# Routing logits by token: the activations as TensorE's stationary operand, the bias added in the same three banks

## What is computed

```
def hier_moe(u, lp):
    x = u.reshape(-1, dm)
    lg = (x @ lp['rt_grp_w'] + lp['rt_grp_b']).astype(F32)
    pg = jax.nn.softmax(lg, axis=-1)
    sel = jnp.argmax(lg, axis=-1)
    ...
    le = (x @ lp['rt_exp_w'] + lp['rt_exp_b']).astype(F32).reshape(-1, N_GROUPS, EXP_PER_GROUP)
```

## Time and profile before

| | |
|---|---|
| median of 3 runs | 1442.87 us (1442.4 to 1446.44) |
| the profiled execution's own time | 1438.41 us |
| span in its profile | 1436.6 us |
| TensorE's mean granted clock in it | 0.929 of 2.4 GHz |
| TensorE busy with matmuls | 1212.6 us |
| VectorE busy | 498.1 us |
| ScalarE busy | 277.2 us |

### The profile page before, as it was taken

The page is one execution under the profiler, slowest core; times in us unless marked ns, Lnnn a source line. Parts: engine busy times, 40 slices in busy tenths (PEclk is TensorE's granted clock), DMA queues, the critical chain, the costliest instruction groups (busy, mean ns, idle before and its releaser), DMA issues. The chain is left out here.

```text
span 1436.6 us, 27279 instructions
## 1 busy us (share of the span) xinstructions
PE 1212.6 (84%) x12154; PEld 784.3 (55%) x12154; DVE 498.1 (35%) x1275; ACT 277.2 (19%) x683; POOL 37.0 (3%) x65
## 2 busy tenths in 40 slices
PE   3789876678788889999978999588789899999974
PEld 3455554667775455455434555368785465455432
DVE  0103058352635260111115033956753350110113
ACT  2012053221320121011001124333320121011002
POOL 2000000000000020000000000000000000000000
PEclk9799986999999989999998999689998989999997
DMA  9754460335251417775716232000001307775711
GB/s 353 208 207 153 171 235 1 127 113 199 84 141 36 140 31 236 250 246 204 234 61 182 90 90 74 1 2 4 9 4 55 121 7 248 255 242 186 246 48 44
DMA packets 135678, 191.74 MB, mean 133 GB/s; under 512 B 16563, under 2 KB 100768, under 8 KB 135168
## 3 DMA queue, kind: packets, MB, share of 16 engines
q1 hardware_dynamic: 132256, 179.32, 38.1%
q0 software_dynamic: 2032, 6.23, 1.4%
q10 hardware_dynamic: 1264, 4.33, 0.8%
HBM read 187.63 MB, written 2.23 MB: 132 GB/s over the span
## 5 line engine op out<-in xcount | busy, mean ns | idle before, releaser
L1125 PE MATMUL bank<-ring,region 128*128 128x512 f32 x512 | 224.8, 593 | 0.0
L1205 ACT ACTIVATE region<-bank 128x256 f32<-128x256 f32 (+5 forms) x318 | 128.8, 430 | 422.9 <-PE bank L1146 105.8
L1125 PEld LDWEIGHTS bank<-ring,region 128*128 128x128 f32 x512 | 96.0, 190 | 112.4 <-issue 110.8
L1961 DVE SCALAR_TENSOR_TENSOR region<-region,bank 128x256 f32<-128x256 f32 x32 | 15.4, 480 | 334.2 <-ACT region L1462 334.2
L1146 PE MATMUL bank<-ring,region 128*128 128x512 f32 x256 | 111.2, 593 | 0.0
L1771 DVE COPY_PREDICATED region<-lev,bank 128x512 f32<-128x512 uint8 (+1 forms) x90 | 61.1, 679 | 121.1 <-PE bank L772 120.6
L967 PE MATMUL bank<-u,ring 128*128 128x384 f32 x288 | 94.9, 487 | 0.0
L1556 DVE SCALAR_TENSOR_TENSOR h<-bank,mod,h 128x128 f32<-128x128 f32 (+1 forms) x160 | 56.4, 411 | 103.8 <-PE bank L1041 62.4
L1041 PE MATMUL bank<-u,ring 128*128 128x384 f32 x256 | 86.4, 500 | 5.9 <-DVE u L1854 5.9
L1146 PEld LDWEIGHTS bank<-ring,region 128*128 128x128 f32 x256 | 48.1, 190 | 57.3 <-issue 57.3
L876 PE MATMUL bank<-ring,cond 128*32 128x128 f32 x1536 | 51.6, 284 | 28.1 <-issue 14.7
(11 more groups left out here) (268 smaller groups left out, 1523.6 us busy)
## 6 DMA issues: line engine op xcount, KB each, us to landing
ring<-in_moe_w SPq DMA_DIRECT2D x96, 1024.0 KB, 6.5
ring<-in_w_mod SPq DMA_DIRECT2D x48, 1024.0 KB, 8.4
ring<-in_w_in SPq DMA_DIRECT2D x20, 768.0 KB, 9.1
ring<-in_w_in SPq DMA_DIRECT2D x12, 256.0 KB, 6.1
region<-in_bands POOLq DMA_DIRECT2D x2, 1280.0 KB, 7.7
ring<-in_w_out SPq DMA_DIRECT2D x4, 576.0 KB, 4.2
ring<-in_w_out SPq DMA_DIRECT2D x8, 288.0 KB, 6.1
ring<-in_w_out SPq DMA_DIRECT2D x6, 384.0 KB, 6.3
```

Source lines behind the costliest of these rows:

```text
L1125: last = pe.matmul(bank[j % 2][:, :], xs[:, job % 2, c, :], w[:, c, :], start=(c == 0), stop=(c == KT - 1))
L1205: return act.activation(dst, src, ACT.Copy)
```

## The change

The operands of the logits' matmuls change places. The stationary operand is now a tile of the activations, `u[:, c, tc(t)]` (128 channels by 128 tokens), and the moving one is `route_w[:, c, :]`, 20 columns. The logits come out by token, 128 partitions by 20, in bank 5 + t for token tile t. The bias's matmul of ones with `route_b` is added to the same accumulation. ScalarE's copy, its two semaphores, the buffer `logits` and the three matmuls with the identity go. Since banks 5, 6 and 7 now hold logits when `u` is transposed, the six groups of transposes go round banks 0 to 4, and the sixth waits until ScalarE has copied the first. VectorE's copy of the logits reads 20 columns of each of three banks instead of 60 of one.

```
@@ -1067,20 +1065,19 @@
                 for c in range(KT):
                     pe.wait_ge(u_up, 2 * KT * l + KT + c + 1)
-                    last = pe.matmul(bank[7][0:20, 0:T], route_w[:, c, :], u[:, c, :], start=(c == 0), stop=(c == KT - 1))
-                last.then_inc(logit_mm, 1)
-                pe.wait_ge(logit_cp, l + 1)
+                    for t in range(NT):
+                        pe.matmul(bank[5 + t][:, 0:20], u[:, c, tc(t)], route_w[:, c, :], start=(c == 0), stop=False)
                 for t in range(NT):
-                    dst = bank[7][:, t * 20:(t + 1) * 20]
-                    pe.matmul(dst, logits[:, tc(t)], ident[0:20, 0:20], start=True, stop=False)
-                    last = pe.matmul(dst, ones_row, route_b[:, :], start=False, stop=True)
+                    last = pe.matmul(bank[5 + t][:, 0:20], ones_row, route_b[:, :], start=False, stop=True)
                 last.then_inc(route_mm, 1)
 
 
                 for g in range(2 * NT):
                     t, half = g // 2, g % 2
+                    if g == 5:
+                        pe.wait_ge(utok_cp, 2 * NT * l + 1)
                     for q in range(4):
-                        last = pe.transpose(bank[g][:, tc(q)], u[:, 4 * half + q, tc(t)], ident)
+                        last = pe.transpose(bank[g % 5][:, tc(q)], u[:, 4 * half + q, tc(t)], ident)
                     last.then_inc(utok_mm, 1)
 
                 pe.wait_ge(onehot_up, l + 1)
@@ -1433,12 +1430,10 @@
                 norm(l, 0)
-                act.wait_ge(logit_mm, l + 1)
-                copy(logits, bank[7][0:20, 0:T]).then_inc(logit_cp, 1)
                 for g in range(2 * NT):
                     t, half = g // 2, g % 2
                     act.wait_ge(utok_mm, 2 * NT * l + g + 1)
-                    copy(u_tok[:, t, 512 * half:512 * half + 512], bank[g][:, :]).then_inc(utok_cp, 1)
+                    copy(u_tok[:, t, 512 * half:512 * half + 512], bank[g % 5][:, :]).then_inc(utok_cp, 1)
@@ -1880,7 +1875,7 @@
                 dve.wait_ge(route_mm, l + 1)
-                link(dve.tensor_copy(rl, bank[7][:, 0:20 * NT].rearrange("p (t n) -> p t n", t=NT)))
+                link(dve.tensor_copy(rl, psum[:, 5:5 + NT, 0:20]))
```

More of the change, by code:

```diff
@@ L283, in build @@
         xs = view(2, KT, P)
-        logits = view(T)[0:20, :]
         silu = view(2, DE)
@@ L323, in build @@
         modt_mm = sem("modt_mm")
-        logit_mm, logit_cp = sem("logit_mm"), sem("logit_cp")
         route_mm, utok_mm, rank_mm, hid_mm, down_mm = (sem("route_mm"), sem("utok_mm"), sem("rank_mm"),
```

## The result

The changed kernel takes 1448.46 us, the median of 11 runs (1442.45 to 1452.45), against 1443.62 for the kernel before in 11 runs beside it. The ratio is 1.0034 with a 95% interval of 1.0018 to 1.0050, so it is slower by 4.9 us, between 2.6 and 7.2. I had forecast the side and the clock in the logits, but 11.1 us.

What follows compares the result with a forecast made beforehand. It took TensorE to bound the kernel, its matmuls filling 84% of the span. Averaging 7.0 and 13.4 us gave 10.2, plus 0.9 for the gather 11.1, on 1442.9: 1454.0 us, range 1446 to 1460.

Steps and rivals of the forecast that it cites:

- with a rise: Case where the clock rises late in the transposes, so rank matmuls run at full clock; 3.3 and 3.7 us by layer.
- without: Case where the clock stays at 0.50 through transposes and rank matmuls; 6.5 and 6.9 us by layer.
- the price of 11.6 us: Logits and bias: 54 records at 0.215 us, clock at 0.50 throughout, up to the first transpose; +1.5 and +1.4 us.
- Rival (2): Logits: 20-column matmuls raise the clock near 509.3 as the old ones did; -2.6 us over both layers, 1440.3 us; chance 0.12.
- The sixth group's wait: Transposes: the sixth group's new wait for ScalarE's first copy costs nothing, as the copy ends before that group starts.
- the three-bank copy: VectorE's copy of the logits: reading three banks instead of one is the same 60 elements, 0.22 us.
- VectorE's onehot: Ahead of the rank matmuls: ready near 517.2 while TensorE transposes until 520.5, so its delay costs nothing.
- so I count on one in one layer of two: Transposes: a clock rise expected in one of the two layers; (7.0 + 13.4)/2 = 10.2 us.
- rival (1): Logits and transposes: clock low, no rise in the transposes of either layer; 13.4 + 0.9 = 14.3 us, 1457.2 us; chance 0.30.
- rival (3): Clock rises late in the logits or in both layers' transposes; 7.0 to 7.9 us; shares the forecast's chance of 0.55.
- the gather's +0.9: Gather: its clock rise comes at the mean of 4.6 us, losing 0.9 us over both layers, bounds 0 and +2.
- a shift of the moment at which the gather begins is passed on whole to the end of the layer: From the gather to the layer's end: nothing behind it has slack in which to lose the shift.

Runs made afterwards that it cites:

- wide: Changed kernel, each logits matmul streaming its 20 columns eight times over, 160 columns, with as many loads; ratio to the kernel before 0.9991.
- warm: Changed kernel plus 7 unread 384-column matmuls in TensorE's wait for the layer norm ahead of the logits; ratio to the kernel before 1.0038.
- pad23: Kernel before plus 23 unread matmuls of 2 columns a layer in TensorE's wait ahead of the logits; ratio 1.0006.
- before_warm_rank: Kernel before plus 7 unread 384-column matmuls ahead of the logits and rank matmuls streaming their 4 columns 32 times over; ratio 0.9995.
- gap: Changed kernel with 160-column logits, 128-column rank matmuls, and unread 384-column matmuls, 7 ahead of the logits and 3 ahead of the gather; ratio to kernel before 0.9980.
- pad13: Kernel before plus 13 unread matmuls of 2 columns a layer in TensorE's wait ahead of the logits; ratio 0.9986.
- wide_warm: Changed kernel with 160-column logits matmuls and 7 unread 384-column matmuls in the wait ahead of the logits; ratio to the kernel before 0.9980.

## Why the forecast held, and where it failed

| step, first / second layer | forecast | measured |
|---|---|---|
| logits' start to the transposes | +1.5 / +1.4 | +1.62 / +1.54 |
| transposes | +2.3 with a rise, +2.6 without | +1.65 / +2.06 |
| rank matmuls' start to the gather's start | -0.5 / 0 with a rise, +2.4 / +2.9 without | +0.05 / +0.20 |
| gather's length | +0.9 in all | -0.06 / -0.21 |
| idle at the untaken branches | nothing | +0.4 / -1.9 |
| sum | +11.1 | +5.4 |

The last column is made from the two traces: 11.75 - 10.13 and 11.75 - 10.21; 524.60 - 520.27 = 4.33 against 2.68, and 4.73 against 2.67; and so on. To the gather's end that is +3.26 and +3.59, 6.85 us; with the branches 5.4, inside the measured 2.6 to 7.2. The medians gave 4.8. The two spans, counted from the first layer's logits, differ by 5.9 us; the 0.5 left over lies behind the idle times.

**Right.** The clock. It stays at 1.2 GHz through the logits and bias, with 48 of their 54 records at 0.214 us, and the price of 11.6 us was 11.75. wide shows that with the same loads more streamed columns bring the rise back, warm that a full clock at the start doesn't save it. Rival (2) is out. The Trainium skill, page "TensorE: Matmul & The Clock Gate", section "LDWEIGHTS (loading the stationary operand)", has a rule on loads that names no clock; by it, as an estimate, the 54 records would take 5.8 us. The trace agrees at 2.4 GHz (0.10 to 0.11 us a record), not at 1.2. The sixth group's wait, the three-bank copy, ScalarE and VectorE's onehot cost nothing, as said.

**Wrong: how often the transposes raise the clock.** The step "so I count on one in one layer of two" put the sum half way to rival (1), 3.2 us too high. The clock rose in the transposes in all four layers seen, 3.4 and 4.3 us after their start in the first trace, and all later steps fall to the branch "with a rise", for which the forecast had 7.0 us. That is what rival (3) says of both layers' transposes; I had kept it as the forecast's lower end only. Without the gather the three steps measured 7.1 us, but that closeness is in part luck: the transposes came out 0.9 us below their two +2.3, the rank matmuls 0.75 above. Rival (1) is out. The Trainium skill, page "TensorE: Matmul & The Clock Gate", section "Part 4: PE-mode transpose", which would have transposes not count for the clock, doesn't fit these float32 ones, which leave one record each: the clock rose while nothing but transposes had run for 3.4 us, behind 54 records under which it had not, and so it did in warm, 4.4 and 4.7 us after their start. The one fall inside transposes, in pad23, came 1.4 us after their start, behind 2.0 us of small matmuls and waits.

**Wrong: the gather's +0.9.** I took the mean delay of four rises as the expected one. The gather's length repeats from trace to trace (7.1 to 7.7 us in all traces of either kernel), and the change moved it by -0.06 and -0.21 us.

**Wrong: "a shift of the moment at which the gather begins is passed on whole to the end of the layer".** Through the experts it was: from the gather's end to the start of the idle time at the branches it is 217.4 us in both layers of both kernels. But the forecast put the change of this idle time at nothing, and it moved by -1.5 us with the change, by -3.2 in before_warm_rank and by +2.7 in gap. The rows on which I rested had ended at 745 us, ahead of it. pad13 shows that added instructions alone bring the 12.3 us. Which property of the code's place sets it is open; I have the packets and the totals, no rule.

Of the 6.2 us between forecast and ratio, the rises make 3.2, the gather 1.2 (0.9 forecast, -0.3 measured) and the branches 1.5; the rest is 0.3.

## What to carry to other kernels

Before making a matmul narrow in its moving operand, look at the granted clock of the stretch: the old, wider form may have been what raised it, and what is lost then shows in the stages behind. If the array must be kept going, repeat the columns through a broadcast or fill TensorE's waits. Neither delayed the stage behind it here, as long as VectorE set the pace and the filling fitted into the wait, as pad23's did not. And where a program branches, measure the idle time at the branch in each version before reading a gain of a few us: added instructions can move it by as much, whatever they compute.

## What the runs showed of the hardware

- With 128 columns loaded, a float32 record costs 0.10 to 0.12 us at 2.4 GHz, with 4 streamed columns (30 in 3.41 us, wide_warm) or 128 (30 in 3.51, gap), and 0.214 us at 1.2 GHz with 20 (48 in 10.28, the changed kernel).
- Under matmuls of 20 columns a clock of 2.4 GHz fell 2.4 and 5 us after their start (warm); at 160 columns a clock of 1.2 GHz rose 5.0 and 5.8 us after it (wide).
- Under float32 transposes alone a clock of 1.2 GHz rose 3.4 to 4.7 us after their start, in six layers of six (the changed kernel twice, warm).
- Passing two untaken branches took TensorE 4.6 to 8.5 us, with three packets of instructions of 16 KB and nothing else moving in the stretches shown.
